# Values as the stationary operand in latent and grouped attention, and expert rows moved only for slots that hold a choice

## What is computed

```
def _attend_block(q, k, v, scale):            # latent and grouped attention
    s = einsum('bqkrd,bskd->bkrqs', q, k) * scale
    p = softmax(s, axis=-1)
    return einsum('bkrqs,bske->bqkre', p, v)

br = stack([o_mla, o_gqa, o_r, o_d], axis=2)  # latent, grouped, retention, differential
merged = sum(gates * einsum('btnw,nwd->btnd', br, w_br), axis=2)

scores = sigmoid(t @ w_router)                # 32 experts, 4 chosen per token, 384 tokens
combine = sum(one_hot(eidx, 32) * w[..., None], axis=1)
gu = einsum('nd,edf->nef', t, w_exp_gu)
a = silu(gu[..., :256]) * gu[..., 256:] * combine
routed = a.reshape(n, 32 * 256) @ w_exp_down.reshape(32 * 256, 1024)
```

## Time and profile before

| | |
|---|---|
| time, median of 3 runs | 2130.18 us (2119.91 to 2142.24) |
| the profiled execution | 2137.14 us, its span 2135.6 us |
| busy share of the span | PE 88%, DVE 53%, ACT 41%, POOL 19% |
| mean granted clock of TensorE | 0.949 of full |
| bytes moved | 457.62 MB, mean 214 GB/s |
| chain that ended last | PE 30%, DMA 8%, DVE 5%, issue 3%, ACT 3%, POOL 1% |

### The profile page before, as it was taken

One profiled execution on the slowest core, in us unless ns is written; L12 is line 12 of the kernel. 1 busy time (PEld: TensorE's weight loads), 2 busy tenths in 40 slices (PEclk: granted clock), 3 DMA queues, 4 the chain that ended last, 5 costly groups with the idle time before them and its releaser, 6 DMA issues.

```text
span 2135.6 us, 26671 instructions
## 1 busy us (share of the span) xinstructions
PE 1878.0 (88%) x8784; PEld 1322.2 (62%) x8784; DVE 1138.8 (53%) x1660; ACT 884.0 (41%) x1510; POOL 397.6 (19%) x381
## 2 busy tenths in 40 slices
PE   6998998999977999999179989889999779999990
PEld 3886666888764665555048866568887545555550
DVE  2345557454445666665533455665444646555655
ACT  3342346433342555554133423563333435555541
POOL 2004211400004122221220051214000031221212
PEclk9999998999989999999689999989999999999995
DMA  8443270643435999998374323607434459999984
GB/s 299 149 133 101 99 239 25 199 166 118 158 125 161 344 377 378 378 375 335 133 277 151 119 94 129 228 16 236 138 119 138 174 183 361 363 369 360 363 300 162
DMA packets 120461, 457.62 MB, mean 214 GB/s; under 512 B 13040, under 2 KB 20880, under 8 KB 88880
## 3 DMA queue, kind: packets, MB, share of 16 engines
q1 hardware_dynamic: 96672, 384.86, 50.3%
q0 software_dynamic: 20192, 65.15, 10.3%
q10 hardware_dynamic: 3504, 6.40, 0.8%
HBM read 411.69 MB, written 44.71 MB: 214 GB/s over the span
## 4 chain that ended last, share of the span: by engine, by line
PE 30%; DMA 8%; DVE 5%; issue 3%; ACT 3%; POOL 1%; SPq 0%; DVEq 0%; ACTq 0%; POOLq 0%
PE psum L1878 17%; DMA W<-in_w_exp_gu 7%; PE psum L1818 6%; PE psum L2123 3%; PE psum L1825 2%; PE psum L1843 1%; DMA W<-in_w_mod 1%; POOL slot_tokens L911 1%; ACT scratch_split L1250 1%; DVE W_split L1377 0%; DVE zf L1800 0%; DVE zf L1616 0%; DMA W<-in_w_in 0%; ACT hT L987 0%; DMA zf<-token_rows,vm 0%
## 5 line engine op out<-in xcount | busy, mean ns | idle before, releaser
L1377 DVE TENSOR_TENSOR W_split<-W,W_split 128x2048 fp32r<-128x2048 f32 (+3 forms) x96 | 224.8, 2344 | 407.4 <-ACT W_split L1018 407.4
L1878 PE MATMUL psum<-W_split,qT_split 128*128 128x512 f32 (+3 forms) x1536 | 404.4, 376 | 9.7 <-ACT hT L987 8.1
L1018 ACT ACTIVATE W_split<-W 128x2048 fp32r<-128x2048 f32 (+3 forms) x96 | 175.9, 1838 | 414.1 <-PE psum L1878 345.1
L1878 PEld LDWEIGHTS psum<-W_split,qT_split 128*128 128x128 f32 x1536 | 283.6, 189 | 59.8 <-ACT hT L987 8.7
L1818 PE MATMUL psum<-W,zf 128*96 128x512 f32 (+1 forms) x560 | 258.7, 605 | 30.2 <-ACT zf L1278 27.1
L1878 PE MATMUL psum<-W_split,scratch_split 128*128 128x512 f32 x864 | 275.7, 391 | 0.6 <-DVE hT_split L1372 0.6
L1768 DVE TENSOR_TENSOR W_split<-W,qT_split 128x2048 fp32r<-128x2048 f32 x64 | 146.7, 2292 | 231.0 <-ACT qT_split L1250 231.0
L1250 ACT ACTIVATE qT_split<-W 128x2048 fp32r<-128x2048 f32 x64 | 122.6, 1915 | 259.3 <-DMA W<-in_w_exp_gu 221.6
L1878 PE MATMUL psum<-W_split,hT_split 128*128 128x512 f32 x576 | 211.0, 394 | 5.8 <-DVE scratch_split L1575 5.8
L2123 PE MATMUL psum<-qT_split,hT_split 128*96 128x512 f32 x512 | 198.9, 450 | 6.3 <-issue 6.3
L2123 PE MATMUL psum<-W_split,hT_split 128*96 128x512 f32 x512 | 202.9, 396 | 0.0
(11 more groups left out here) (315 smaller groups left out, 2635.6 us busy)
## 6 DMA issues: line engine op xcount, KB each, us to landing
W<-in_w_exp_gu SPq DMA_DIRECT2D x128, 1024.0 KB, 11.0
W<-in_w_exp_down SPq DMA_DIRECT2D x64, 1024.0 KB, 9.6
W<-in_w_in SPq DMA_DIRECT2D x60, 1024.0 KB, 5.2
W<-in_w_mod SPq DMA_DIRECT2D x48, 1024.0 KB, 4.9
y_slots<-zf SPq DMA_DIRECT2D x64, 384.0 KB, 8.7
W<-in_w_br SPq DMA_DIRECT2D x16, 1024.0 KB, 5.1
y_slots<-kT POOLq DMA_DIRECT2D x2, 6144.0 KB, 33.4
W<-in_w_out SPq DMA_DIRECT2D x8, 1024.0 KB, 5.0
```

Of the source, the lines that this page charges most:

```text
L1018: nc.scalar.activation(high(j), piece(SPLITS[j]), ACT.Copy).then_inc(S["high_ready"], 1)
L1377: V.tensor_tensor(piece(SPLITS[j], Wr), piece(SPLITS[j]), high(j).bitcast(F32), ALU.subtract).then_inc(S["low_ready"], 1)
L1878: ins = nc.tensor.matmul(bank(job, piece_size(key)[1]), act_part[:, k0 + k, t * P:(t + 1) * P], w_part[:, k, :], start=first and (k, i) == ...
```

## The change

Three edits.

1. In `ma`, `mb` and `g` the product with the values is turned round (`weigh_turned`): the values are the stationary operand (128 x 64) and the transposed map streams (128 columns). The output has channels in partitions: a pair of heads fills the 128 partitions of one bank, three token tiles lie side by side, and ACT copies a pair's bank to SBUF once (`empty_pair`), six maps at a time. The division by the sum can no longer be done on the way out, so DVE divides the exponentials in SBUF in place (`scale_map`), before PE transposes them; the transposes wait for that (`p_scaled`). Two banks are set aside for the outputs, the ring has the other five.
2. The outputs of the first two branches are then transposed already, and their `oT` blocks are left out; ACT and DVE split them from SBUF.
3. In the expert part each slot carries two numbers, its token and its choice (token x 4 + k). Slots without a choice carry a number out of bounds, and an indirect DMA leaves such rows out. The gather does so, and the write of results becomes an indirect DMA of POOL into `y_rows`, in the order of choices. So the last gathers become three plain loads of 2 MB from SP into the weights' buffer, which start when all writes have landed, and the zeroing of spare slots goes.

```diff
@@ plan_jobs, softmax_maps
             if i >= 4:
-                jobs.add(("O",) + m[i - 4], "dve")
+                key = ("O",) + m[i - 4]
+                if ends_pair(m[i - 4]):
+                    jobs.add(key, "act", BANK_O[m[i - 4][1] // 2 % 2])
+                else:
+                    jobs.add_part(key, BANK_O[m[i - 4][1] // 2 % 2])
...
-        if g == "mb":
-            jobs.turn_over(BANK_MOD)
+        jobs.turn_over(BANK_O[0])
         softmax_maps(g)
+        if g == "ma":
+            jobs.turn_over(8)
...
     for n in range(NBR):
-        for k in range(4):
+        for k in range(4 if n >= TURNED_BRANCHES else 0):
             jobs.add(("oT", n, k), "dve")
@@ SP, after the loop
-            write_rows(turn, e)
...
                     for e in range(2):
-                        write_rows(turns - 1, e, (0, LESS["dve"][e]))
+                        sp.wait_ge(S[f"y_written{e}"], turns * 16 + 16)
+                        sp.sem_inc(S["sp_steps"], 1)
+                    for t in range(T):
+                        src = a["y_rows"][t * P * TOPK:(t + 1) * P * TOPK].rearrange("(p k) n -> p (k n)", k=TOPK)
+                        sp.dma_start(ybuf[:, t].rearrange("p k n -> p (k n)"), src).then_inc(S[f"y_landed{t}"], 16)
@@ POOL
-                    nc.gpsimd.memset(zero_row, 0.0).then_inc(S["zeros_ready"], 1)
-                    pool.wait_ge(S["zeros_ready"], 1)
-                    pool.dma_start(a["y_slots"].rearrange("(p i) n -> p i n", i=NT)[:, NE:, :],
-                                   zero_row[0:CAP, None, :].to_broadcast([CAP, NT - NE, D])).then_inc(S["zeros_out"], 16)
...
+                    def write_rows(turn, e, less=0):
+
+                        pool.wait_ge(*job_emptied(turn, e, "y0"))
+                        pool.sem_inc(S["gathers"], 1)
+                        pool.wait_ge(*job_emptied(turn, e, "y1", less))
+                        pool.sem_inc(S["gathers"], 1)
+                        nc.gpsimd.tensor_copy(out_index[0:CAP, e:e + 1], of_tile(turn * 2 + e, 1)).then_inc(S["out_index_copied"], 1)
+                        pool.wait_ge(S["out_index_copied"], turn * 2 + e + 1 + AHEAD)
+                        pool.sem_inc(S["gathers"], 1)
+                        pool.indirect_dma_start(a["y_rows"], bass.IndirectOffsetOnAxis(ap=out_index[0:CAP, e:e + 1], axis=0),
+                                                yrow[0:CAP, e, :], None, bounds_check=T * P * TOPK - 1, oob_is_err=False
+                                                ).then_inc(S[f"y_written{e}"], 16)
...
                         pool.indirect_dma_start(xg[0:CAP, e, :], None, a["token_rows"],
-                                                bass.IndirectOffsetOnAxis(ap=index[0:CAP, e:e + 1], axis=0)).then_inc(S[f"x_landed{e}"], 16)
+                                                bass.IndirectOffsetOnAxis(ap=index[0:CAP, e:e + 1], axis=0),
+                                                bounds_check=T * P - 1, oob_is_err=False).then_inc(S[f"x_landed{e}"], 16)
...
                             gather(turn * 2 + e + 4, e, turn + 3)
-
+                            write_rows(turn, e)
@@ ACT
                                 if i >= 5:
-                                    act.wait_ge(*emptied(("O",) + m[i - 5]))
+                                    act.wait_ge(S["p_scaled"], SCALED_AT[m[i - 5]])
...
+                            if i >= 4 and ends_pair(m[i - 4]):
+                                empty_pair(m[i - 4])
...
+                        nc.scalar.activation(dst, bank(key, T * P).rearrange("p (t n) -> p t n", t=T), ACT.Copy).then_inc(S["act_emptied"], 1)
@@ DVE
+                    def scale_map(m, i):
+
+                        r, n = i % 5, P * len(keys_of(m[i][2]))
+                        p = Pb[:, (i % 3) * 384:(i % 3) * 384 + n]
+                        dve.wait_ge(*emptied(("S",) + m[i]))
+                        link(V.reciprocal(rrec[:, r:r + 1], rsum[:, r:r + 1]))
+                        V.tensor_scalar(p, p, rrec[:, r:r + 1], None, ALU.mult).then_inc(S["p_scaled"], 1)
...
-                            if i >= 4:
-                                key, s = m[i - 4], (i - 4) % 5
-                                dve.wait_ge(*emptied(("S",) + key))
-                                link(V.reciprocal(rrec[:, s:s + 1], rsum[:, s:s + 1]))
-                                dve.wait_ge(*filled(("O",) + key))
-                                V.tensor_scalar(out_cols(*key), bank(("O",) + key, HD), rrec[:, s:s + 1], None,
-                                                ALU.mult).then_inc(S["dve_emptied"], 1)
+                            if 1 <= i < len(m) + 1:
+                                scale_map(m, i - 1)
@@ PE
-                                pe.wait_ge(*emptied(("S",) + m[j]))
+                                pe.wait_ge(S["p_scaled"], SCALED_AT[m[j]])
...
+                        multiply(psum[HD * (h % 2):HD * (h % 2) + HD, J.bank(key), t * P:(t + 1) * P],
+                                 [(values(g, h, kt), PTb[:, s * 384 + b * P:s * 384 + (b + 1) * P])
+                                  for b, kt in enumerate(keys_of(t))]).then_inc(S["psum_filled"], 1)
```

More of the change, by code:

```diff
@@ L141, in add, with add_part @@
         self.last[self.banks[key]] = key
+    def add_part(self, key, bank):
+        assert key not in self.number
+        self.number[key] = len(self.number)
+        self.banks[key] = bank
+        self.before[key] = self.last.get(bank)
     def filled(self, key):
@@ L159, with ends_pair @@
 MAPS = attention_maps()
+def ends_pair(mp):
+    return mp[1] % 2 == 1 and mp[2] == T - 1
 def scores_at(g, i):
@@ L177 @@
 BANK_MOD = 7
+BANK_O = 5, 6
 MOD_COLS = (0, D, 3 * D, 4 * D)
@@ L187 @@
 H1_EARLY, H1_BEFORE = 6, (5, 6, 7)
+TURNED_BRANCHES = 2
 def plan_jobs():
@@ L342 @@
             MAX_AT[_key] = len(MAX_AT) + 1
+SCALED_AT = {}
+for _g in ("ma", "mb", "g"):
+    for _m in MAPS[_g]:
+        SCALED_AT[_m] = len(SCALED_AT) + 1
 GATES = [(n, c, t) for n in range(NBR) for c in range(2) for t in range(T)]
@@ L918, in gather @@
                     def gather(tile, e, n):
-                        col = tokens[0:CAP, tile:tile + 1] if isinstance(tile, int) else tokens[0:CAP, bass.ds(tile, 1)]
-                        nc.gpsimd.tensor_copy(index[0:CAP, e:e + 1], col).then_inc(S[f"index_copied{e}"], 1)
+                        nc.gpsimd.tensor_copy(index[0:CAP, e:e + 1], of_tile(tile, 0)).then_inc(S[f"index_copied{e}"], 1)
                         pool.wait_ge(S[f"index_copied{e}"], n)
@@ L936, in _ @@
                             gather(turn * 2 + e + 4, e, turn + 3)
+                            write_rows(turn, e)
                     for e in range(2):
[L939 to L945 removed]
+                        write_rows(turns - 2, e)
+                    for e in range(2):
+                        write_rows(turns - 1, e, LESS["dve"][e])
                     pool.wait_ge(S["cache_out"], 16 * 8)
[L947 removed]
                 @block.scalar
@@ L1700, in _ @@
                     for t in range(T):
-                        ins = V.tensor_scalar(token_f[:, t:t + 1], const[:, K_POS + 3:K_POS + 4], float(t * P), None, ALU.add)
+                        token = const[:, K_POS + 3:K_POS + 4]
+                        V.tensor_scalar(choice_f[:, t * TOPK:(t + 1) * TOPK, 0], token.to_broadcast([P, TOPK]), float(t * P), None, ALU.add)
+                        ins = V.scalar_tensor_tensor(choice_f[:, t * TOPK:(t + 1) * TOPK, 1], token.to_broadcast([P, TOPK]), float(TOPK),
+                                                     iota[:, 0:TOPK], ALU.mult, ALU.add)
                     link(ins)
-                    link(V.tensor_copy(token_u, token_f))
+                    for t in range(1, T):
+                        ins = V.tensor_scalar(choice_f[:, t * TOPK:(t + 1) * TOPK, 1], choice_f[:, t * TOPK:(t + 1) * TOPK, 1], float(t * P * TOPK), None,
+                                              ALU.add)
+                    link(ins)
+                    link(V.tensor_copy(choice, choice_f))
                     def product(gu, s, n):
@@ L1797, in _ @@
                     post_gains(1)
-                    for i in range(T * TOPK):
-                        dve.wait_ge(S[f"y_landed{i % 6}"], 16 * (i // 6 + 1))
-                        V.scalar_tensor_tensor(acc[:, i // TOPK], ybuf[:, i % 6], weight[:, i:i + 1], acc[:, i // TOPK], ALU.mult,
-                                               ALU.add).then_inc(S["summed"], 1)
-                        dve.wait_ge(S["summed"], i + 1)
-                        if i % TOPK == 1 and i > TOPK:
-                            residual(acc, 1, i // TOPK - 1)
+                    for t in range(T):
+                        dve.wait_ge(S[f"y_landed{t}"], 16)
+                        for k in range(TOPK):
+                            i = t * TOPK + k
+                            V.scalar_tensor_tensor(acc[:, t], ybuf[:, t, k], weight[:, i:i + 1], acc[:, t], ALU.mult, ALU.add).then_inc(S["summed"], 1)
```

(3 more changed lines are left out.)

95 lines of the change are left out of this document (51 added, 44 removed).

## The result

The changed kernel takes 2175.75 us in the median of four runs (2164.04 to 2182.01), the kernel before 2127.8 beside it: 1.021 times as long, 95% interval 1.0171 to 1.025. The forecast was 2121, with a range up to 2147. The profiled execution took 2178.89 us, span 2177.2, with a mean granted clock of 0.937 (0.949 before).

A forecast was written before the change was run, and what follows sets the result against it. The prediction saw PE and DMA limits almost level in the expert loops, and PE limiting attention and gates. Loop -24, tail +10, gates -3 and attention +8 made -9 us, from 2130.18 to 2121 us; range 2101 to 2147.

The forecast's parts named there:

- PE's product streams 128 columns instead of 64: 0 us: Attention's product with the values: the wider stream costs 0 us, at most 0.05 a map (3 us in all).
- Attention, the scaling: DVE's scaling in SBUF waits for POOL in "ma": 4 us a layer, 8 in all; 0 to 2 elsewhere.
- Gates, -3 us: Gates: eight transposed blocks of three a layer leave PE, in sum 3 us gained.
- The loop, -24 us: Expert loops: row traffic halves, PE then limits; intervals fall to 10.05 and 10.2 us, 24 us gained, bounds 30.6 and 0.
- rival 2: Expert loop: empty slots in the upper partitions leave half the DMA engines fully loaded; loop -3, total 2144 us; chance 0.17.
- Its other form: Expert loop, rival 2: a left-out slot costs as much as a moved one, with the same outcome.
- The tail, +10 us: Layer's tail: three 2 MB loads bring x 5 us later a layer, 10 in two layers (6 to 14).
- The layer's end, 0 us: Layer's end: POOL's twelve issues go, but they lay under DVE's sums; 0 us.
- The sum: Whole kernel: loop -24, tail +10, gates -3, attention +8, together -9 us, giving 2121 us.
- Rival 3: Port lock: each scaling in "ma" waits a whole POOL product, 30 us, and PE's clock stays down; 2149 us; chance 0.13.

The follow-up runs named there:

- e5: Changed kernel with two heads' values as a 128 x 128 operand and POOL's gate-start products after branch 0's low parts: 2126.7 us, ratio 0.9985.
- e6: e5 with DVE's scaling of the exponentials left out: 2136.12 us, ratio 1.0029; its trace has 66 gathers instead of 64.
- e4: Changed kernel with POOL's six products at the gates' start waiting until DVE has written branch 0's low parts: 2148.65 us, ratio 1.007.
- e9: Kernel before with the third edit alone, empty slots filled with numbers within bounds so all 96 rows are moved: 2124.04 us, ratio 0.9967.
- e7: Kernel before with the third edit alone, a tile's choices put into every second partition: 2110.28 us, ratio 0.991.
- e10: e7 with POOL waiting at its end for the layer's last sum, as in the kernel before: 2120.51 us, ratio 0.9955.

## Why the prediction was wrong, point by point

- **Attention, "PE's product streams 128 columns instead of 64: 0 us".** This step failed, by 27 us. I compared one group of four records by its duration (0.61 us), and those two groups had the same stationary shape. The change also makes the stationary operand 64 columns wide, and that alters the array's tile, which no row that I chose shows, though the trace did (`64*128` behind transposes, 0.43 against 0.33 us). The duration of a group hides it; the distance between starts does not.
- **Attention, the scaling.** I took it for the main cost, 8 us with bounds 0 and 30. In "ma" it took 288 to 1187 ns, median 420, so some of them are held up, as forecast. What the cured kernels still lose up to the low part is 8.5 us (754.0 against 745.5), and e5 against e6 gives 6 us for the scaling. The size is right, the place is not: I had put 4 us a layer into "ma" and 0 to 2 into the rest, but without the scaling "mb" and grouped attention are 1.2 us a layer shorter, and "ma" is not shorter in the first layer and 1.3 us in the second.
- **Gates, -3 us.** The gain is there: 234.8 to some 233.1 us a layer where the clock stays up, 3.4 us in both. (The first layer of the kernel before took 238.7, with 6.8 us at the lower clock.) What failed is the step "ACT and DVE split them from SBUF", which I costed at nothing. I had named the shared port for the scaling and did not ask the same of the split, whose input moved from PSUM to SBUF beside POOL's longest products. That cost 26 us (13.2 a layer by e4), of which 18.0 are PE's gaps (9.20 and 8.85) and most of the rest the lower clock behind them.
- **The loop, -24 us.** Measured -15.4 from first to last gather, -19.5 over the 27 intervals that I had counted (273.2 and 278.0). That it came so near is luck. The base of the second layer was 10 us too high, an accident of that execution; the left-out rows give only 3.7 us a loop (280.0 to the mean 276.3). Spread over the partitions they give 8.9, all that PE leaves. So rival 2 described what happens to more than half of the saving: empty slots bunched in the upper partitions. Its other form is out: with all rows moved (e9) a loop takes 279.7 us. My text also has 1536 choices in 64 tiles; they are 1536 in the 32 tiles of each layer, and the 48 slots a tile that I went on with are right.
  The Trainium skill, DMA: Bandwidth & Descriptors, section The descriptor swizzle, deals the partitions of a 128-partition transfer to the engines by position; e7, with 96 partitions, agrees in its effect, though no view here shows the sixteen engines apart.
- **The tail, +10 us.** Measured +11.8, first sum 16.4 us after the last result (forecast 15), x after 42.1 (forecast 41). Right.
- **The layer's end, 0 us.** It gave back 10. I had costed POOL's twelve issues as covered by DVE, which was so, but not that POOL would be free at the end of the layer.
- **The sum.** The terms measured above come to +27 (tile) +8 (rest of attention) +26 (split) -3 (gates) -15 (loop) +12 (tail) -10 (ends) = +45, against 41.6 in the two traces. The difference lies within what a stage varies from run to run: the kernel before alone had 4 us of lower clock in its gates.
- **The rivals.** Rival 3 came nearest in time (2149), but not for its reason. Two things that it names did happen, elsewhere or smaller: the lock decides at the split, not at the scaling, and the clock was lower in "ma".

## What to carry to other kernels

Turning a product round changes three things: which operand streams, the shape of the array's tile, and in which memory the result is found by its next reader. Cost each of them; a narrow stationary operand among full ones costs PE at every change, and filling its width with columns that nobody wants can be cheaper. Compare starts with starts, and look up the granted clock of a stage before a loss is put down to instructions. When an operand moves from PSUM to SBUF, look at what POOL does at that moment. Here it paid to spread the rows that a DMA leaves out over the partitions (5 us a loop).

## What the runs showed that I had not expected

- A change between `128*128` and `128*64` keeps the weight load from running ahead: about 0.15 us a change, 0.28 us a map of "ma", invisible as idle time of PE. One between `128*128` and `96*128` costs nothing.
- PE's gap of 8.9 us was followed by a stretch at the lower clock, in both layers: 36 products took 10.85 us instead of 8.32.
- A DVE subtraction of 384 columns took 0.55 us from PSUM or alone, and up to 3.86 us with both inputs in SBUF beside a POOL product of 1536 columns.
- One wait at POOL's end for work that DVE finishes anyway keeps the next layer back by 8.0 us (17.7 in e10 against 9.7 in e7), and the end of the program by 6.3.
